# A two-layer diffusion step: the first norm's statistics kept as 128x5 numbers, its modulation made in two halves

## The reference, cut to what matters

```python
def rms_norm(x, g):
    xf = x.astype(jnp.float32)
    xf = xf * lax.rsqrt(jnp.mean(xf * xf, axis=-1, keepdims=True) + EPS)
    return (xf * g.astype(jnp.float32)).astype(x.dtype)

def adaln(cond, w, b):                      # w: 1024 x 6144
    return jnp.split(jax.nn.silu(cond) @ w + b, 6, axis=-1)

# in each layer, for both groups of tokens
sh1, sc1, g1, sh2, sc2, g2 = mod
h = rms_norm(x, p['norm1']) * (1 + sc1) + sh1
... = jnp.split(h @ p['w_in'], offs, axis=-1)   # ten column groups; the kernel begins with mla_cq, 256 columns
... four mixers, output projection, a second norm (sh2, sc2), squared-ReLU MLP
```

## Time and profile before

| | us |
|---|---|
| median of three runs (lowest, highest) | 1745.99 (1741.97, 1748.03) |
| the profiled execution's own time | 1742.77 |
| its span | 1740.6 |
| PE busy in it | 1605.6 (92%) |
| DVE busy | 943.9 (54%) |
| ACT busy | 664.5 (38%) |
| POOL busy | 148.5 (9%) |

### The profile page before, as it was taken

The page is one execution under the profiler, slowest core; times in us unless marked ns, Lnnn a source line. Parts: engine busy times, 40 slices in busy tenths (PEclk is TensorE's granted clock), DMA queues, the critical chain, the costliest instruction groups (busy, mean ns, idle before and its releaser), DMA issues.

```text
span 1740.6 us, 28317 instructions
## 1 busy us (share of the span) xinstructions
PE 1605.6 (92%) x11686; PEld 1488.4 (86%) x11686; DVE 943.9 (54%) x1480; ACT 664.5 (38%) x1045; POOL 148.5 (9%) x107
## 2 busy tenths in 40 slices
PE   5878997899999999999988789888999999999998
PEld 3755895589999999999967579856999999999998
DVE  3654346846555545554584534486566456554553
ACT  4555534654322322232244554356433222332231
POOL 1003103410000000000010130153000000000000
PEclk8988998999999999999999999989999999999999
DMA  9540443312232222223634206431222222222211
GB/s 309 163 138 1 72 143 116 98 38 60 73 97 63 70 87 73 73 73 111 196 106 135 85 1 129 128 123 49 73 74 73 73 73 73 73 73 73 89 57 61
DMA packets 150856, 160.14 MB, mean 92 GB/s; under 512 B 16390, under 2 KB 132808, under 8 KB 150728
## 3 DMA queue, kind: packets, MB, share of 16 engines
q1 hardware_dynamic: 150024, 158.13, 29.6%
q10 hardware_dynamic: 576, 0.16, 0.0%
q0 software_dynamic: 128, 0.05, 0.0%
HBM read 153.41 MB, written 4.65 MB: 91 GB/s over the span
## 4 chain that ended last, share of the span: by engine, by line
PE 79%; DVE 11%; ACT 5%; issue 2%; DMA 1%; POOL 1%; ACTq 0%; DVEq 0%; SPq 0%; POOLq 0%
PE ps L1548 33%; PE ps L1890 26%; PE ps L1641 10%; PE ps L1528 1%; PE ps L1695 1%; PE ps L1613 1%; PE ps L1717 1%; PE ps L1664 1%; DVE extrema L1302 1%; PE ps L1574 1%; ACT pt_c L787 1%; POOL pr_a L751 1%; DMA ada_own<-in_w_ada 1%; DVE extrema L1285 1%; PE ps L1684 1%
## 5 line engine op out<-in xcount | busy, mean ns | idle before, releaser
L787 ACT ACTIVATE w_hi<-w_raw 128x2048 fp32r<-128x2048 f32 (+1 forms) x90 | 169.9, 1887 | 335.7 <-PE ps L1548 324.3
L1344 DVE SCALAR_TENSOR_TENSOR xT<-ps,mod,xT 128x128 f32<-128x128 f32 (+2 forms) x432 | 190.0, 440 | 195.7 <-PE ps L1548 183.8
L1131 DVE TENSOR_TENSOR w_lo<-w_raw,w_hi 128x2048 fp32r<-128x2048 f32 (+1 forms) x90 | 203.1, 2257 | 139.4 <-ACT w_hi L787 138.0
L1890 PE MATMUL ps<-xa_hi,w_hi 128*128 128x320 f32 (+1 forms) x1024 | 236.1, 312 | 0.0
L1890 PE MATMUL ps<-xa_lo,w_hi 128*128 128x320 f32 (+1 forms) x1024 | 235.2, 311 | 0.0
L1890 PE MATMUL ps<-xa_hi,w_lo 128*128 128x320 f32 (+1 forms) x1024 | 235.1, 311 | 0.0
L1548 PE MATMUL ps<-z_hi,w_hi 128*128 128x320 f32 x1024 | 233.9, 309 | 0.9 <-DVE xT L1344 0.9
L1548 PE MATMUL ps<-z_lo,w_hi 128*128 128x320 f32 x1024 | 233.3, 309 | 0.0
L1548 PE MATMUL ps<-z_hi,w_lo 128*128 128x320 f32 x1024 | 233.3, 309 | 0.0
L1103 ACT ACTIVATE z_relu<-z_relu,z_shift 128x128 f32<-128x128 f32 (+1 forms) x128 | 72.2, 564 | 307.0 <-DVE z_relu L1448 304.9
L1890 PEld LDWEIGHTS ps<-xa_hi,w_hi 128*128 128x128 f32 x1024 | 173.5, 189 | 0.3
(11 more groups left out here) (241 smaller groups left out, 2350.2 us busy)
## 6 DMA issues: line engine op xcount, KB each, us to landing
w_raw<-in_mlp_w SPq DMA_DIRECT2D x64, 1024.0 KB, 5.3
ada_own<-in_w_ada SPq DMA_DIRECT2D x54, 512.0 KB, 4.5
w_raw<-in_w_in SPq DMA_DIRECT2D x14, 1024.0 KB, 8.3
ada_mix<-in_w_ada SPq DMA_DIRECT2D x21, 512.0 KB, 7.5
ada_room<-in_w_ada SPq DMA_DIRECT2D x15, 512.0 KB, 8.9
w_raw<-in_w_out SPq DMA_DIRECT2D x8, 768.0 KB, 5.2
ada_first<-in_w_ada SPq DMA_DIRECT2D x6, 512.0 KB, 9.2
x_in<-in_x_sample SPq DMA_DIRECT2D x1, 2048.0 KB, 9.0
```

The costliest lines, as they stand in the source:

```text
L787: do(nc.scalar.activation(out, in_, ACT.Copy), sem)
L1131: do(V.tensor_tensor(w_lo[:, n % 2, 0:w], w_raw[:, n % 2, 0:w], f32(w_hi[:, n % 2, 0:w]), ALU.subtract), w_lo_ready)
L1344: do(V.scalar_tensor_tensor(dst, src, gate[:, m:m + 1], dst, ALU.mult, ALU.add), sem if last else None)
L1890: last = M.matmul(bank(b + a_, s1 - s0), w[r][:, k, c:c + P], x[:, k, s0:s1], start=k == 0 and q == 0, stop=k == KC - 1 and q == 2)
```

## The change

Per layer, in the order in which it acts:

- **Sums per token on the partitions.** PE takes the squares as weights and a single column of ones as moving operand (ten products, five token tiles times two sources) and leaves 128x5 numbers in one bank. `mean`, `root_x` and `invert` work on `tok_rstd`, 128x5, a part of the tile `few`.
- **Spread.** The new `spread_rstd` multiplies `tok_rstd`'s columns, broadcast to 128x128, with pieces of the identity: six products, 128 or 64 columns wide. That gives the reciprocal root on all partitions, 640 wide, in PSUM banks 6 and 7; ACT copies it to `rstds[0]` (`take_rstd`). POOL and DVE wait for that copy.
- **Ticks.** PE's sums now stand behind ticks 0 to 3 in both layers (before: behind ticks 0 to 7 in layer 0), the spread behind ticks 4 to 7. The units' order of columns is 0, 2, 1, 3 in groups of four chunks, so that turn 1 gives the first half of the scale. `scales` runs twice, for chunks 0 to 3 after turn 1, and for 4 to 7 after turn 3, which DVE now does in the middle of `h_of`. The units' sums go to banks 2 and 1 in turn, so that a unit need not wait for the copy of the row before.
- **Order on ACT and SP.** In layer 0 the table load for the root stands ahead of the squares. ACT's `split_hi(0)` stands behind the copy of the spread root, DVE's `split_lo(0)` behind `invert`. On SP the first projection's weights are loaded ahead of the last six units of `w_ada`.
- **DVE's wait for the tables.** The line `dve.wait_ge(const_dma, 64)` is not moved in the text, but layer 0's `mean`, `invert` and the rest, which stood ahead of it, are now behind it, inside the loop.
- **After the projection.** The five banks of `project_cq` are 4, 5, 0, 6, 7. The first token tile of the next projection (`ckv`) runs ahead of the four late ticks, which wait until ACT has read all five banks.

```diff
@@ psum_steps, acc_banks @@
-        acc += [(l, "sum1", "dve")]
+        acc += [(l, "sum1", "dve"), (l, "rstd", "act")]
...
-CQ_BANKS = (0, 1, 3, 7, 2)
+CQ_BANKS = (4, 5, 0, 6, 7)
+ADA_GROUPS = (0, 2, 1, 3)
@@ sync @@
             sp.wait_ge(t_done, KC)
+            load_weights(0)
             load_adas(0, range(AFTER_X, 16))
-            load_weights(0)
             sp.dma_start(rope_d[:, :, :, :], a["rope_d"]).then_inc(const_dma, 16)
@@ gpsimd @@
-                pool.wait_ge(rstd_ready, nrm + 1)
+                l = nrm // 2
+                pool.wait_ge(m_act, acc_ix.last_reader(acc_ix.at[(l, "rstd")])[1])
@@ scalar @@
+            def take_rstd(l):
+
+                i = acc_ix.at[(l, "rstd")]
+                act.wait_ge(m_done, i + 1)
+                do(nc.scalar.activation(rstds[0][:, :].rearrange("p (a n) -> p a n", a=2), acc_view(i), ACT.Copy), m_act)
+
+            def first_norm(l):
+
+                load_sqrt()
+                for c in range(KC):
+                    if l:
+                        act.wait_ge(y_read, (l * GROUPS - 1) * KC + c + 1)
+                    square_x(2 * l, c)
+                ada_ticks(48 * l, range(4))
+                root_x(2 * l)
+                ada_ticks(48 * l, range(4, 8))
+                take_rstd(l)
+                if l == 0:
+                    split_hi(0)
+                ada_ticks(48 * l, range(8, 12))
+                h_halves(2 * l, range(1))
+                ada_ticks(48 * l, range(12, 18))
+                h_halves(2 * l, range(1, KC))
@@ scalar, in h_halves @@
-                act.wait_ge(acol_ready, nrm + 1)
                 for c in chunks:
+                    act.wait_ge(acol_ready, 3 * l + 1 + c // 4)
@@ vector @@
+                if which == 0:
+                    do(V.tensor_scalar(tok_rstd, bank(acc_banks(i), NT), 1.0 / D, EPS, ALU.mult, ALU.add), m_dve)
+                    return
...
-                rstd = rstds[nrm % 2]
+                rstd = rstds[1][:, :] if nrm % 2 else tok_rstd
                 dve.wait_ge(sqrt_ready, nrm + 1)
-                do(V.reciprocal(rstd[:, :], rstd[:, :]), rstd_ready)
+                do(V.reciprocal(rstd, rstd), None if nrm % 2 else tok_ready)
@@ vector, in h_of @@
+                dve.wait_ge(m_act, acc_ix.last_reader(acc_ix.at[(l, "rstd")])[1])
...
                 for c in range(KC):
+                    if c == 3:
+                        ada_ticks(48 * l, range(12, 17))
+                    if c == 4:
+                        ada_tick(48 * l, 17)
+                        scales(nrm, 4, 4)
@@ vector, the program @@
             for c in range(KC):
                 add_square(0, c)
-            ada_ticks(0, range(6))
-            mean(0)
-            invert(0)
-            ada_ticks(0, range(6, 14))
-            split_lo(0)
-            ada_ticks(0, range(14, 18))
             dve.wait_ge(const_dma, 64)

             for l in range(DEPTH):
                 U = 45 * l
-                if l:
-                    mean(2 * l)
-                    ada_ticks(48 * l, range(6))
-                    invert(2 * l)
-                    ada_ticks(48 * l, range(6, 18))
+                mean(2 * l)
+                ada_ticks(48 * l, range(6))
+                invert(2 * l)
+                if l == 0:
+                    split_lo(0)
+                ada_ticks(48 * l, range(6, 12))
+                scales(2 * l, 0, 4)
                 late = 48 * l + 16
-                ada_ticks(late, late_ticks(l, 0))
-                scales(2 * l)
                 h_of(l)
@@ tensor @@
+            def spread_rstd(l):
+
+                begin_acc((l, "rstd"))
+                pe.wait_ge(tok_ready, l + 1)
+                b = acc_banks(acc_ix.at[(l, "rstd")])
+                for t in range(NT):
+                    for s, e in ((P * t, P * t + P),) if t != 2 else ((P * t, HALF), (HALF, P * t + P)):
+                        last = M.matmul(bank(b + s // HALF)[:, s % HALF:s % HALF + e - s],
+                                        tok_rstd[:, t:t + 1].broadcast_to([P, P]), ident[:, s - P * t:e - P * t],
+                                        start=True, stop=True, skip_group_check=True)
+                last.then_inc(m_done, 1)
+
+            def first_norm(l):
...
+                ada_ticks(48 * l, range(4))
+                begin_acc((l, "sum1"))
+                sums(l, "sum1")
+                ada_ticks(48 * l, range(4, 8))
+                if l:
+                    pe.wait_ge(y_read, did["y"])
+                spread_rstd(l)
+                ada_ticks(48 * l, range(8, 18))
...
                 project_cq(l, U)
+                project(l, U + 1, "ckv", range(1))
+                pe.wait_ge(p_read, proj_at[(l, "cq", NT - 1)] + 1)
+                pe.wait_ge(ada_reduced, 12 * l + 4)
                 ada_ticks(late, late_ticks(l, 1))
-                project(l, U + 1, "ckv")
+                project(l, U + 1, "ckv", range(1, NT))
```

More of the change, by code:

```diff
@@ L504, in ada_banks, with ada_acc_bank @@
         def ada_banks(first):
-            return (6, 6) if first % 48 == 32 else (2, 3) if first % 48 == 0 and first else (4, 5)
+            return (6, 6) if first % 48 == 32 else (2, 3) if first % 48 == 0 else (4, 5)
+        def ada_acc_bank(first, k):
+            return (2, 1)[k // 4 % 2] if first % 48 == 0 else ada_banks(first)[0]
         def ada_ticks_of(first):
@@ L809, in ada_tick @@
                         act.wait_ge(ada_turned, u // 4)
-                    copy(ada_row[:, :], bank(ada_banks(first)[0]), ada_rows)
+                    copy(ada_row[:, :], bank(ada_acc_bank(first, unit[1])), ada_rows)
             def ada_ticks(first, ks):
@@ L1568, in ada_tick @@
                     if u % 4 == 0 and u:
-                        pe.wait_ge(ada_rows, u // 4)
+                        pe.wait_ge(ada_rows, u // 4 - (first % 48 == 0 and unit[1] >= 4))
                         if b_acc == b_turn and unit[1]:
                             pe.wait_ge(ada_reduced, u // 4)
-                    c = 512 * b_acc + AC * (u % 4 // 2)
+                    c = 512 * ada_acc_bank(first, unit[1]) + AC * (u % 4 // 2)
                     for j in range(AR):
@@ L1587, in sums @@
                 rstd = rstds[nrm % 2]
+                if which == "sum1":
+                    out = bank(acc_banks(acc_ix.at[(l, which)]), NT)
+                    pe.wait_ge(sum_used, (KC - 2) * (nrm + 1))
+                    pe.wait_ge(sq_ready, KC * (nrm + 1))
+                    for t in range(NT):
+                        M.matmul(out[:, t:t + 1], rstd[:, P * t:P * t + P], ones[:, 0:1], start=True, stop=False,
+                                 skip_group_check=True)
+                        last = M.matmul(out[:, t:t + 1], sq[:, (KC - 1) % 2, P * t:P * t + P], ones[:, 0:1],
+                                        start=False, stop=True, skip_group_check=True)
+                    last.then_inc(m_done, 1)
+                    return
                 out = acc_view(acc_ix.at[(l, which)])
@@ L1746, in _ @@
             pe.wait_ge(cond_ready, 1)
-            ada_ticks(0, range(8))
-            begin_acc((0, "sum1"))
-            sums(0, "sum1")
-            ada_ticks(0, range(8, 18))
             for l in range(DEPTH):
```

68 lines of the change are left out of this document (23 added, 45 removed).

## The result

The changed kernel takes 1753.81 us (median of 7 runs, 1751.33 to 1759.81), the kernel before 1744.01 on the same chip (7 runs, 1741.60 to 1748.03). The ratio is 1.0056, with a 95% interval of 1.0042 to 1.0069: slower, by 9.8 us. The prediction was 1751, range 1743 to 1757, with "slower" its likeliest outcome. The profiled execution took 1755.15 us, its span is 1753.0.

A forecast was written before the change was run, and what follows sets the result against it. Bound: the chain of waits, 79% held by TensorE, so the start of PE's next product counts. Layer 0 +6.1 + 0.4, layer 1 -1.6 + 0.4: +5.3 us on the median 1745.99, so 1751; range 1743 to 1757.

The forecast's parts named there:

- rival C: One-column products leave TensorE slow through units 4 to 7, and landing is nearer 6.3 us: +10, 1756 us; chance 0.1.
- The wait: Layer 0: DVE's wait for four tables, now ahead of the mean, starts it at 41.5 us instead of 34.64.
- landing: Layer 0: `col_mask` lands 3.5 us after its issue, with 2.3 and 6.3 us as bounds.
- mean to projection: Layer 0: from the mean at 41.5 us through spread, split and coefficients to the projection's start at 56.8 us.
- Sums and units: Layer 0 on PE: sums 3.3 us, half at full clock (bounds 1.1, 4.4); units 4 to 7 with turn 0 2.9.
- SP's queue: Layer 0: from unit 15's issue to `col_mask`'s 3.2 us, being 4.11 less 0.92 for the moved weights.
- Behind the start: Both layers: `acol`'s second half hidden, else up to 1.5 us more; 0.4 us per layer for ACT's copies before `ckv`.
- Layer 1: No table outstanding: net 1.6 us gained ahead of the projection (bounds 0 and 3.5), 0.4 us lost behind it.
- the 2.9 us for `hf`: Layer 1: `hf` of chunk 0 not through before POOL's two products end at 895.5; started 898.43, so 2.9 us earlier.
- The reciprocal: Falls from 4.15 to about 0.30 us; in layer 1 what it saves goes to PE's spread behind four units.
- The shared port: DVE and GpSimd lock each other out: `acol` and `hf` wait for POOL's products; layer 1 gains 1.6, otherwise 3.2 us.
- The price of a one-column product: On PE: each record of the sums takes 0.11 us at full clock, 0.22 at half.

The follow-up runs named there:

- experiments 1: The changed kernel with DVE's wait for the four tables moved back behind the first half of `acol` in layer 0; 1747.35 us. Also called gate_back.
- experiment 2: The kernel before, with only the wait for the four tables moved ahead of layer 0's first turn and mean; 1750.83 us. Also called Before_gate.
- experiment 5: gate_table with 96 columns of ones per product of the sums instead of one, same records and weight loads; ratio 0.9990 to the kernel before.
- experiment 9: The changed kernel, wait included, with only the column of ones of the sums' products made 96 wide; 1752.42 us.
- Before_gate: The kernel before, with only the wait for the four tables moved ahead of layer 0's first turn and mean; 1750.83 us.
- experiment 6: gate_table with reciprocal ahead of turn 0's reduction, spread behind units 4 and 5, ACT's copy ahead of units 4 to 7's rows; ratio 0.9990 to the kernel before.
- experiment 8: gate_table with the edits of experiment 5 and experiment 6 together; 1742.35 us. Also called wide_spread.
- experiment 7: gate_table with POOL starting its products only behind DVE's first two chunks of `hf`; ratio 1.0014 to the kernel before.
- whole_coef: wide_spread with turns 0 to 3 and all of `acol` ahead of the first chunk of `hf`; 1750.54 us.
- gate_back: The changed kernel with DVE's wait for the four tables moved back behind the first half of `acol` in layer 0; 1747.35 us.
- gate_table: gate_back with layer 0's table load for the root behind the squares and the first row's copy; ratio 1.0005 to the kernel before.
- wide_spread: gate_table with 96 columns of ones and the spread moved ahead in PE's queue, both edits together; 1742.35 us.

## Why the prediction was right, and where its sizes were off

**What was right and what was luck.** The time lies in the range and the forecast mechanism was found, but the rise was under-forecast: 5.3 us, measured 9.8. The distance of 1751 to 1753.81 is smaller than that because the median of the three first runs, 1745.99, on which the forecast stood, was 2 us above the 1744.01 of seven; that is luck. The +10 us of rival C is nearer in number, with half of its mechanism. The stated range, 1743 to 1757, is also 1 us below the bounds that were worked out for it, 1744 and 1758, without a reason.

**The wait (right).** The mechanism that decided the forecast is the one that experiments 1 and 2 show. The mean was forecast at 41.5 us and came at 43.09. The terms:

| step of layer 0 | predicted | measured |
|---|---|---|
| squares end, table load ahead of them | 28.6 | 28.4 |
| sums take | 3.3 | 4.3 |
| units 4 to 7 and turn 0 take | 2.9 | 4.5 |
| SP, unit 15 to `col_mask` | 3.2 | 1.9 |
| landing | 3.5 | 3.8 |
| mean to projection | 15.3 | 15.2 |
| behind the projection's start | +0.4 | +1.9 |

*Sums and units.* I let half the sums and nearly all units run at full clock. The stretches of the changed kernel (columns as above) show the low level all through the sums and through most of the units:

```profile
28.50:32.90 4.40, 4.40 (x24) 4.38 (x28) 0.00 (x0) 0.48 (x1) 0.00 (x0) 0.50 1.09 348
32.90:37.40 4.50, 4.41 (x37) 1.84 (x36) 0.00 (x0) 0.00 (x0) 0.00 (x0) 0.57 0.65 208
```

The 4.4 us that I had as the upper bound of the sums was the true value, and the 4.5 us of the units lie above their upper bound of 4.1. Rival C had this mechanism; it held in the clock and not in the landing, which stayed near the forecast's 3.5. In layer 1, experiments 5 and 9 show the cause. In layer 0 PE comes from a hole of 5.06 us, and the sums run at the low level with the wide column too; experiment 9 has the units behind them faster, which agrees with the cause without setting it apart from the hole.

*SP's queue.* The issues from unit 15 to the mask are 0.37 to 0.51 us long; the 3.2 us taken from the earlier trace rows came to 0.8 each. Before_gate, with the old list, has 0.49 to 0.58, so those rows were of an execution in which SP was slow, for a reason that stays open. This error hid half of the first two, which is luck as well.

*Behind the start.* The prediction cost the second half of `acol` at nothing, "hidden, and if it were not, up to 1.5 us more". It was not hidden: 1.49 us for the small sum beside POOL's third product, and PE waited 1.93 and 0.56 us inside the projection. About half of that comes back. In the kernel before, the projection's first twenty records ran at the low clock, 0.21 us apart instead of 0.12:

```profile
50.70:55.00 4.30, 4.26 (x20) 4.29 (x21) 4.16 (x5) 4.10 (x7) 1.69 (x1) 0.50 0.90 303
```

Net, the projection itself takes 1.3 us more, and what follows it 0.6 instead of 0.4.

**Layer 1 (wrong in sign).** Forecast −1.6 and +0.4, measured +1.0. Two terms failed. The units behind the sums cost 1.6 us more, at the low clock (I had 2.6 us from the trace of before, where wide products stood ahead of them). So the projection started 0.3 us earlier instead of 1.6. And behind its start come 1.3 us instead of 0.4: 0.7 in the projection, which I had at nothing, and 0.6 behind it. Experiment 9 sets the two apart: with the wide column in the change itself the projection starts 1.9 us earlier, near the forecast, behind it come 1.4 us, and layer 1 is at 61.31, 0.5 under the kernel before. So the sign hinges on the clock. A slip of the working is also in the 2.9 us for `hf`: it set the end of POOL's two products (895.5) against the old start of `hf` (898.43). Measured, `hf` starts 2.2 us earlier, before those products end, and is stretched.

**The reciprocal (right in both).** It fell to 0.19 us, and that bought little. In layer 0 the wait covers it; in layer 1 what it saved went to PE's queue, in which the spread stands behind four units. Experiments 6 and 8 bring part of it out again: 1.9 and 2.4 us in layer 0 (8 against 5), 0.4 in layer 1 in both.

**The shared port (right).** `acol`'s sum and `hf` took 1.05 and 3.51 us beside POOL. The Trainium skill (SBUF — State Buffer, section Who interferes with whom) calls DVE's and GpSimd's pair an exclusive lock. By experiment 7 the traces agree: 0.17 and 2.31 with POOL held back, and 2.4 us turned up at the next operation.

**The price of a one-column product (right).** 0.11 us at the full clock, as taken from the earlier trace rows, and 0.21 at half. The Trainium skill (TensorE: Matmul & The Clock Gate, section LDWEIGHTS) has a load cost its columns over 1.2 GHz, 107 ns for 128; the rows at full clock agree, and 96 columns instead of one do not change the pace. At the low clock the same record took twice that figure. The gap of about 25 ns for 1 to 64 columns that the Trainium skill gives on the same page, section Back-to-back issue gap, is not what bound here. (The 1.7 us that the prediction took from it fit layer 1's term of 2.2; layer 0's term was 3.3.)

**What stays open.** The rest of the program, with the same work, took from 1591.5 us (whole_coef) to 1603.5 (gate_back) in the twelve profiled executions, more than any section differs. So the difference of a few experiments' medians (gate_back and gate_table above all) is not accounted for by their sections, and I cannot tell whether the first norm has any part in that. The medians are evidence for the wait; for the smaller steps the evidence is the sections.

## What to carry to other kernels

When an operation is shortened or moved, look at what waits stand ahead of it in the new order: one line on transfers that nobody needed yet cost more than all the arithmetic saved. Price a new chain at the engine that it queues on, since a result of 0.19 us is worth nothing while its consumer stands behind four other jobs. Where TensorE's work is made of tiny products, compare the granted clock behind it with that of before, and try wider products that cost nothing before giving the idea up.

## What the runs showed of the hardware that was not expected

- Twenty matmul records of one column, each with a weight load of 128 columns, kept PE busy for 2.2 us without a gap, and the granted clock then fell to half: 0.60 over the next 4.3 us. With 96 columns and the same loads it stayed at 1.00.
- These products took the same time with 96 columns as with one: 0.11 us at the full clock, 0.21 at half, so the weight load halves its pace with the clock too. The spread's twelve records took 1.60 us at the full clock and 2.93 at half.
- A hole of 4.74 us on PE was followed by 4.5 us at a granted clock of 0.50, a hole of 1.73 us by none. A hole of 2.55 us, in layer 1 of the change, was followed by 0.61 over 4.2 us, and one of 1.82 us, in layer 0 of wide_spread, by 0.57 over 3.8 us, so the length of the hole alone doesn't decide it. Shortening a hole of PE can be worth more than its own length.
- Holding POOL back freed two DVE operations and blocked a third, by slightly more: 1.05 to 0.17 and 3.51 to 2.31, but 1.14 to 3.53.
- The landing of a 48 KB table took 3.7 us where the 1 MB of weights had left SP's queue ahead of the last units, and 5.7 to 6.3 us where they left just ahead of the tables.
